# Norms moved into the expert programs, a first block with small loads only, and a result stored in eight parts

## The reference

```
def rmsnorm(x, g):
    xf = x.astype(F32)
    y = xf * lax.rsqrt(jnp.mean(xf * xf, axis=-1, keepdims=True) + EPS)
    return (y * g.astype(F32)).astype(x.dtype)
...
x -> x + mixer_i(rmsnorm(x, g[2i]))        (i = 0..3: SSD, NSA, HGRN2, SSD)
x -> x + experts_i(rmsnorm(x, g[2i+1]))
```

## Time and profile before

| | |
|---|---|
| median of three runs | 2247.63 us |
| the profiled execution, its own time | 2249.39 us |
| its span, first to last instruction | 2247.3 us |
| PE busy | 2070.9 us (92%) |
| DVE busy | 782.3 us (35%) |
| ACT busy | 593.4 us (26%) |
| mean granted clock of PE | 0.951 |
| bytes read from HBM | 600.31 MB |

### The profile page before, as it was taken

One profiled execution on the slowest core, in us unless ns is written; L12 is line 12 of the kernel. 1 busy time (PEld: TensorE's weight loads), 2 busy tenths in 40 slices (PEclk: granted clock), 3 DMA queues, 4 the chain that ended last, 5 costly groups with the idle time before them and its releaser, 6 DMA issues. The chain is left out here.

```text
span 2247.3 us, 29946 instructions
## 1 busy us (share of the span) xinstructions
PE 2070.9 (92%) x11027; PEld 1344.5 (60%) x11027; DVE 782.3 (35%) x1852; ACT 593.4 (26%) x1335; POOL 116.6 (5%) x96
## 2 busy tenths in 40 slices
PE   4999989997999768989997999989997999989998
PEld 3877854443777346754444879654443877864443
DVE  2489222222012136332222242232222489422221
ACT  2477121111111114321112332121112377221111
POOL 0133000000100000000000000000000133100000
PEclk9999999999999869999998998799998999999999
DMA  6788479997737646289996445289996688569996
GB/s 229 216 302 253 150 299 421 422 421 268 230 117 251 198 140 242 98 343 421 421 422 240 150 144 160 100 354 421 421 421 241 198 284 279 161 245 422 421 421 248
DMA packets 248711, 629.03 MB, mean 280 GB/s; under 512 B 14008, under 2 KB 175976, under 8 KB 198680
## 3 DMA queue, kind: packets, MB, share of 16 engines
q1 hardware_dynamic: 231000, 608.59, 72.7%
q10 hardware_dynamic: 15232, 10.49, 1.6%
q0 software_dynamic: 2368, 8.48, 1.1%
HBM read 600.31 MB, written 35.56 MB: 283 GB/s over the span
## 5 line engine op out<-in xcount | busy, mean ns | idle before, releaser
L1491 PE MATMUL bank<-ring,e_xg 128*64 128x512 f32 x1536 | 336.6, 594 | 0.0
L684 PE MATMUL bank<-uT,ring 128*128 128x264 f32 x1280 | 298.0, 392 | 0.0
L684 PEld LDWEIGHTS bank<-uT,ring 128*128 128x128 f32 x1280 | 243.4, 192 | 47.5 <-issue 6.8
L1491 PEld LDWEIGHTS bank<-ring,e_xg 128*64 128x64 f32 x1536 | 107.5, 137 | 211.1 <-issue 202.4
L1519 PE MATMUL bank<-e_late,e_hT 128*64 128x512 f32 x1024 | 226.8, 595 | 2.7 <-ACT e_hT L1631 2.7
L1395 DVE TENSOR_TENSOR xT<-xT,bank 128x264 f32<-128x264 f32 x256 | 109.9, 429 | 225.4 <-PE bank L1542 221.9
L1627 ACT ACT_TABLE_LOAD x32 | 41.1, 1283 | 459.5 <-PE bank L1491 459.5
L1387 DVE TENSOR_TENSOR e_hg<-e_sg,bank 128x512 f32<-128x512 f32 x32 | 22.0, 688 | 389.1 <-PE bank L1491 389.1
L1519 PEld LDWEIGHTS bank<-e_late,e_hT 128*64 128x64 f32 x1024 | 70.7, 137 | 134.8 <-issue 127.9
L2783 PE MATMUL bank<-uT,ring 128*128 128x264 f32 x512 | 124.3, 404 | 6.1 <-PEq L213 6.1
L1467 PE MATMUL bank<-e_to_row,e_u_nat 128*128 128x128 f32 x1024 | 126.1, 278 | 0.0
(11 more groups left out here) (475 smaller groups left out, 2328.1 us busy)
## 6 DMA issues: line engine op xcount, KB each, us to landing
ring<-in_moe_w SPq DMA_DIRECT2D x192, 1024.0 KB, 10.2
e_late<-in_moe_w SPq DMA_DIRECT2D x192, 1024.0 KB, 12.2
ring<-in_m_w_in SPq DMA_DIRECT2D x40, 1024.0 KB, 9.0
s_hbuf<-in_ssm SPq DMA_DIRECT2D x32, 512.0 KB, 5.5
out_ssm_s<-s_hbuf SPq DMA_DIRECT2D x32, 512.0 KB, 3.4
ring<-in_m_w_out SPq DMA_DIRECT2D x16, 1024.0 KB, 6.9
ring<-in_h_w_in SPq DMA_DIRECT2D x16, 1024.0 KB, 8.2
n_page<-in_cache_cmp SPq DMA_DIRECT2D x48, 256.0 KB, 3.9
```

The costliest lines, as they stand in the source:

```text
L684: mm = nc.tensor.matmul(bank[p % 3][0:m, 0:T], lhs, uT[:, k], start=(k == 0), stop=(k == KT - 1))
L1491: mm = nc.tensor.matmul(bank[b][CAP * j:CAP * j + CAP, :], xg[:, EK // 2 * h + k, CAP * j:CAP * j + CAP], rows_of(key)[:, k], start=(h + k ...
```

## The change

Five edits, all shown below:

1. `W.send(sp, SLOTS)` leaves the first block. It now stands in the block of the first norm, so the ring loads are issued after the small loads have landed and the barrier has been passed.
2. The block for `lb` is gone. Its instructions stand at the head of `hgrn_layer`, on DVE and ACT. The tiles `lb`, `lbm` and `lbe` are now local there.
3. `norm_all` becomes `first_norm`, for layer 0 alone. It has eight squares of one tile and a buffer of eight tiles, and a Sqrt of one column ahead of the squares, which brings Sqrt's table.
4. The norms of layers 1 to 3 stand at the end of both expert programs (`square_x` on ACT, `sum_x` on PE, `norm_x` on DVE). The square of tile c waits for the last addition to that tile.
5. In layer 3, ACT stores tile c of `xT` as a DMA of its own (132 KB), issued once its last addition is made. The last block only waits.

```diff
@@ first block @@
                 sp.dma_start(w_rt[:, 0:4 * KT * 20], I["w_rt"].rearrange("p a k c -> p (a k c)")).then_inc(*in_loaded.one())
-                W.send(sp, SLOTS)
                 sp.wait_ge(*in_loaded.now())
...
+        def first_norm():
...
+                    @block.sync
+                    def _(sp):
+                        W.send(sp, SLOTS)
+
                     @block.scalar
                     def _(act):
...
+                        nc.scalar.activation(rs[:, 0:1], eps[:, 0:1], ACT.Sqrt)
+                        for c in range(KT):
+                            nc.scalar.activation(sq[:, c], xT[:, c], ACT.Square).then_inc(*act_done.one())
+                        act.wait_ge(*pe_done.at(1))
+                        nc.scalar.activation(rs[:], bank[0][:, 0:T], ACT.Sqrt, bias=eps[:, 0:1], scale=1.0 / D).then_inc(*act_done.one())
...
@@ last block @@
-                sp.dma_start(O["yT"], xT[:]).then_inc(*out_sent.one())
-                sp.wait_ge(*out_sent.now())
+                for name in ("out_sent", "misc_dma"):
+                    sp.wait_ge(*core.count(name, 16).now())
@@ moe @@
+        def store_y(act, sent, ended):
+
+            for c in range(KT):
+                act.wait_ge(*ended(c))
+                act.dma_start(O["yT"][:, c], xT[:, c]).then_inc(*sent.one())
+
+        def square_x(act, norm, b, ended):
+
+            for c in range(KT):
+                act.wait_ge(*ended(c))
+                if c == 0:
+                    nc.scalar.activation(x_rs[:, 0:1], eps[:, 0:1], ACT.Sqrt)
+                nc.scalar.activation(x_sq[:, c], xT[:, c], ACT.Square).then_inc(*norm["x_squared"].one())
+            act.wait_ge(*norm["x_norm_step"].at(1))
+            nc.scalar.activation(x_rs[:], bank[b][:, 0:T], ACT.Sqrt, bias=eps[:, 0:1], scale=1.0 / D).then_inc(*norm["x_norm_step"].one())
+
+        def sum_x(pe, norm, b):
+
+            for c in range(KT):
+                pe.wait_ge(*norm["x_squared"].at(c + 1))
+                mm = nc.tensor.matmul(bank[b][:, 0:T], ones, x_sq[:, c], start=(c == 0), stop=(c == KT - 1))
+            mm.then_inc(*norm["x_norm_step"].one())
+
+        def norm_x(dve, norm):
+
+            dve.wait_ge(*norm["x_norm_step"].at(2))
+            nc.vector.reciprocal(x_rs[:], x_rs[:]).then_inc(*norm["x_norm_step"].one())
...
+                nc.vector.scalar_tensor_tensor(out=uT[:, c], in0=xT[:, c], scalar=par("norm_g", (layer * 2 + 2) * 8 + c), in1=x_rs[:],
+                                               op0=ALU.mult, op1=ALU.mult).then_inc(*norm["x_norm_step"].one())
...
@@ gathered_program of ACT @@
-                    leave(act, dense_total, (silu_done, comb_spread, u_copied))
+                    if layer < 3:
+                        square_x(act, norms[0], 4, lambda c: x_added.at(4 + KT * (PAIRS - 1) + c + 1))
+                    else:
+                        store_y(act, y_sent[0], lambda c: x_added.at(4 + KT * (PAIRS - 1) + c + 1))
+                    leave(act, dense_total, (silu_done, comb_spread, u_copied, *only(norms[1], "x_squared"), *stored(1)))
```

More of the change, by code:

```diff
@@ L346, in _ @@
                 link(nc.vector.memset(w_rt[:, 4 * KT * 20:], 0.0))
[L347 to L369, removed]
@@ L392, in _ @@
                             pe.wait_ge(*act_done.at(c + 1))
[L393 to L396, removed]
+                            mm = nc.tensor.matmul(bank[0][:, 0:T], ones, sq[:, c], start=(c == 0), stop=(c == KT - 1))
+                        mm.then_inc(*pe_done.one())
@@ L1264, in moe @@
         comb_made = count("comb_made")
+        y_sent = [count("out_sent", 16), count("misc_dma", 16)]
+        norms = [{name: count(f"{name}_{way}") for name in ("x_squared", "x_norm_step")} for way in ("gathered", "dense")]
         dense_total = {h_filled: 4 * NE, y_filled: 8 * NE, comb_turned: 1, silu_done: 4 * NE, h_used: 4 * NE + 2, weighted: 4 * NE + 2,
@@ L1270, in moe, with only, stored @@
                           to_row_ready: PAIRS - 1, comb_done: 7, dec_gathered: 2, dec_kept: 2, xg_copied: 2 * PAIRS}
+        if layer < 3:
+            x_sq = sb("x_sq", [128, KT, T])
+            x_rs = sb("x_rs", [128, T])
+            for c, total in (("x_squared", KT), ("x_norm_step", KT + 3)):
+                gathered_total[norms[0][c]] = dense_total[norms[1][c]] = total
+        if layer == 3:
+            for way, totals in zip(y_sent, (gathered_total, dense_total)):
+                totals[way] = 16 * KT
+        def store_y(act, sent, ended):
[3 more added lines that the diff above has]
+        def square_x(act, norm, b, ended):
+            for c in range(KT):
+                act.wait_ge(*ended(c))
[5 more added lines that the diff above has]
+        def sum_x(pe, norm, b):
+            for c in range(KT):
+                pe.wait_ge(*norm["x_squared"].at(c + 1))
[4 more added lines that the diff above has]
+            nc.vector.reciprocal(x_rs[:], x_rs[:]).then_inc(*norm["x_norm_step"].one())
+            dve.wait_ge(*norm["x_norm_step"].at(3))
+            for c in range(KT):
+                nc.vector.scalar_tensor_tensor(out=uT[:, c], in0=xT[:, c], scalar=par("norm_g", (layer * 2 + 2) * 8 + c), in1=x_rs[:],
+                                               op0=ALU.mult, op1=ALU.mult).then_inc(*norm["x_norm_step"].one())
+        def only(norm, *names):
+            return tuple(norm[name] for name in names) if layer < 3 else ()
+        def stored(way):
+            return (y_sent[way],) if layer == 3 else ()
         def leave(eng, totals, counts):
@@ L2955, in keep_rows @@
                     nc.scalar.copy(oT[:, 2 * j:2 * j + 2, 0:LP], bank[3 + j][:].rearrange("p (h t) -> p h t", h=2)).then_inc(*o_kept.one())
+                act.wait_ge(*lb_dve.at(5))
+                nc.scalar.activation(lbe[:], lbe[:], ACT.Exp).then_inc(*lb_act.one())
                 for p in range(VT + 1):
@@ L3061, in update @@
                     add.then_inc(*s_done.one())
+                bound = linker(dve, lb_dve)
+                lbv = par("h_lb", 0, 32)
+                bound(V.tensor_reduce(lbm[:], lbv.rearrange("p (l c) -> p c l", l=4), AX.X, ALU.max))
+                for l in range(4):
+                    bound(V.tensor_tensor(lbe[:, 8 * l:8 * l + 8], lbv[:, 8 * l:8 * l + 8], lbm[:], ALU.subtract))
+                dve.wait_ge(*lb_act.at(1))
+                bound(V.tensor_reduce(lbm[:], lbe[:].rearrange("p (l c) -> p c l", l=4), AX.X, ALU.add))
+                bound(V.reciprocal(lbm[:], lbm[:]))
+                bound(V.tensor_tensor(lb[:, 0:8], lbe[:, 8:16], lbe[:, 16:24], ALU.add))
+                bound(V.tensor_tensor(lb[:, 0:8], lb[:, 0:8], lbm[:], ALU.mult))
+                bound(V.tensor_scalar(lb[:, 8:16], lb[:, 0:8], -1.0, 1.0, ALU.mult, ALU.add))
                 for h in range(HH):
```

55 lines of the change are left out of this document (29 added, 26 removed).

## The result

| | before | after |
|---|---|---|
| median of four runs | 2247.74 us | 2211.57 us (2209.80 to 2214.05) |
| the profiled execution | 2249.39 us | 2212.78 us |
| its span | 2247.3 us | 2210.9 us |
| mean granted clock of PE | 0.951 | 0.951 |

The ratio after to before is 0.9839, with a 95% interval of 0.9823 to 0.9854. The forecast was 2213.7 us, 2.1 above the median.

A forecast was written before the change was run, and what follows sets the result against it. PE was taken to bound the expert blocks, so only its idle pieces, 98.8 us, could shrink. Gains of 12.5 (start), 16.8 (passages) and 4.6 (end) sum to 33.9 us: 2213.7 us from the median 2247.63, with 2205 to 2225 for 8 in 10.

The forecast's parts named there:

- The start: Before layer 0: PE's first mixer matmul starts at 24.0 us instead of 36.57, a gain of 12.5 us.
- the ends: First norm: its eight sum matmuls on PE take between 3.83 us and 6.0 us, depending on the clock.
- The rival that SP holds the first block: At the start: issuing the ring takes SP 16.81 us wherever it stands; start gains 8.1, time 2218.1 us; chance 0.14.
- The passages: Three ways from experts to the next mixer: 5.5, 5.5 and 5.8 us gained, together 16.8 us.
- Only DVE's branch is late now; PE, ACT and SP wait at the barrier. I take 3.2: Between DVE's norm and the next mixer: leaving the expert block, branch and barrier, still costs 3.2 us.
- the way out vanishes: Leaving the expert blocks: DVE's branch is served while PE sums; passages gain 25 us, time 2205.5 us; chance 0.06.
- The lower end for one passage: One passage from experts to mixer: at least 3.7 us gained, with 3.74 and 0.4 paid and 1 us more at half clock.
- The end: Behind the last addition: eight stores by ACT end the span at 2242.7 instead of 2247.3 us, a gain of 4.6 us.
- The mixers: Mixer blocks of all layers: no lengthening counted; zero taken for late conv0, at worst 2 us.
- A mixer's block is longer than before by more than 1 or 2 us: Mixer blocks in the profile after: a sign named in advance that would show the prediction wrong.
- The sum: Whole kernel: gains of 12.5, 16.8 and 4.6 us make 33.9 us, giving 2213.7 us against the median.
- my own case: Whole kernel: the main forecast of 33.9 us gained, 2213.7 us against the median; chance 0.74.

The follow-up runs named there:

- the repeat: The changed kernel run once more with nothing altered; 2214.57 us, ratio 0.9848 to the kernel before.
- store_only: The kernel before with only the result stored in eight parts by ACT; 2246.03 us, ratio 0.9986 to the kernel before.
- act_leaves_last: The changed kernel with ACT waiting, before it leaves the expert program, for DVE's last tile of the norm; 2211.54 us.
- norms_only: The kernel before with only the norms of layers 1 to 3 moved into the expert programs; 2229.65 us, ratio 0.9914 to the kernel before.
- after_pe_without_dense: The changed kernel with PE's part of the dense program, never run on these inputs, left out; 2215.44 us, ratio 0.9849 to the kernel before.
- pe_without_dense: The kernel before with PE's part of the dense program, never run on these inputs, and its branch left out; 2239.7 us, ratio 0.9952.

## Why the prediction was right, and where it was not

**The start** (12.5 forecast, 12.4 found, 11.3 in the repeat's trace): right in its steps. Small loads in by 10.5, issues that no longer take 16.8 us, a sum of 5.7 us between the ends, PE at 24.2. The rival that SP holds the first block is refuted: six issues took 11.59. Their queue was empty at the first, which fits; no run tested the queue alone.

**The passages** (16.8 forecast, 26.2 found): the failed step is "Only DVE's branch is late now; PE, ACT and SP wait at the barrier. I take 3.2". It takes the 3.74 of before for DVE's. Those were PE's branch (542.48 to 546.83 in the trace before), which now runs under PE's own sums and DVE's reciprocal, and DVE's own branch isn't late either: it comes 2.7 us before its last tile. What is left is 0.39 us. It was the rival "the way out vanishes", given 0.06, for a reason close to the right one: what is served early is PE's branch too, not only DVE's. The lower end for one passage, 3.7, should have been 3.6 by its own terms (561.40 less 552.7, 3.74, 0.4 and 1). The rest of the term held: the norm of DVE ended 8.8 us behind the additions, the sums ran without a gap, and the mixer began slow as expected (0.74 in its first 10 us), though behind 6.1 us of idle time and not 9.

**The end** (4.6 forecast, 4.4 found): the size is right. The eight stores overlapped: 132 KB each and 5.15 us for all issues, SP waiting 0.5 at the end. The rule that stood against the edit, from the Trainium skill (DMA: Bandwidth & Descriptors, Measured and Anatomy of one DMA), is DMAs of at least 1 MB and 2.0 us of fixed cost for each, measured there with DMAs that GpSimd issues. The trace does not show that cost paid one after the other. The 2.7 us that the prediction gave ACT for its branch and barrier were PE's: before, PE's branch ended at 2240.99; now ACT's takes 0.05 us, and PE, whose branch ends at 2209.43, is the last that the last block waits for, by 0.2 us over ACT.

**The mixers** (no cost forecast): wrong. "A mixer's block is longer than before by more than 1 or 2 us" was named as what would disprove me, and NSA's is longer by 5.4 us. The prediction took every mixer's length as fixed, and that is the step that failed. It is the clock: with the same 469 DVE instructions of NSA set side by side, each step of over 0.5 us by which after falls behind lies in one of its stretches at 1.2 GHz or within 3 us behind it. The table gives, for some kernels, the time that PE spent at 1.2 GHz within that layer (its length times one less the granted clock, doubled), beside the layer's length.

| | NSA at 1.2 GHz | NSA | HGRN2 at 1.2 GHz | HGRN2 |
|---|---|---|---|---|
| store_only | 109 | 650.7 | 47 | 479.5 |
| act_leaves_last | 89 | 648.8 | 62 | 484.4 |
| before | 91 | 647.6 | 64 | 486.7 |
| after | 114 | 652.9 | 70 | 488.7 |
| norms_only | 115 | 653.9 | 69 | 488.1 |
| after_pe_without_dense | 118 | 659.9 | 70 | 488.7 |

HGRN2 follows the clock closely, 9.2 us over 23 more at half rate. NSA follows it loosely (7 us between 114 and 118), since it matters what lies in a slow stretch: in the first 27.0 us of the longest (770.7 to 797.7 in after) PE is busy 13.0. The code of these layers is the same except for `lb` at HGRN2's head, which `norms_only` does not move.

Is it the shorter passage that lowers the clock? `pe_without_dense` says no: its passages take 13 us, and its NSA 653.0. The 14 us that begin 256 us behind NSA's first matmul, for before, after and `pe_without_dense`:

```profile
817.40:831.40 14.00, 13.47 (x90) 8.41 (x92) 4.39 (x12) 3.19 (x5) 0.00 (x0) 0.76 0.07 24
796.16:810.16 14.00, 11.98 (x57) 8.01 (x56) 4.00 (x6) 1.60 (x3) 0.00 (x0) 0.50 0.00 0
814.13:828.13 14.00, 11.98 (x56) 8.13 (x56) 4.00 (x6) 1.92 (x6) 0.00 (x0) 0.50 0.00 1
```

The repeat and `norms_only` show 0.50 there as well. Nor is it pure chance of an execution. Counted from NSA's first matmul, the repeat's stretches at 1.2 GHz begin and end within 0.2 us of after's. `act_leaves_last`, with passages as short as 9.6, has others, and took 648.8. The runs of one kernel do spread: before's went from 2243.13 us at a clock of 0.953 to 2254.85 at 0.945. That is 1.5 us for each 0.001 of clock, for the same program. So the loss is the clock's, it does not hang on the length of the passage, and what puts the slow stretches where they are stays open.

**The sum**: forecast 33.9, found 36.4 in span. The two errors, 9.4 us too little for the passages and 6.7 lost in the mixers, have opposite signs. The total was right within 2.5 us partly by luck, and a chance of 0.74 for my own case was too high: its mechanism at the passages was not what happened.

## What to carry to other kernels

At the end of a block, ask for each engine when it leaves and how long its own branch takes, and let the one with the longest branch leave first. Here ACT leaving last added 0.4 to 0.8 us to a passage, and PE 4.1 to 4.4. And where PE idles ahead of a stage that it bounds, unread matmuls can pay, as long as they wait for nothing that would hold its branch and no other engine's late data takes the gain back. A sum of terms that comes out can still hide terms that did not: check each one.

## What the runs showed of the hardware

- PE's branch over the skipped program takes 3.3 to 4.6 us, ACT's and DVE's 0.04 to 0.06. It runs while PE's queued matmuls still execute, and DVE's ran 2.7 us ahead of its last tile.
- Six issues of 1 MB loads took 11.59 us from an empty queue and 16.81 behind six small loads.
- An issue by ACT took 0.34 to 0.51 us for seven of the eight stores of after, and 1.57 for the seventh.
- 12 unread matmuls (5.5 us of PE) bring PE's mixer from a granted clock of 0.74 to 1.00 in its first 10 us.
- Counted from NSA's first matmul, the slow stretches of two executions of one program lay within 0.2 us of each other.
- The same program ran at mean clocks from 0.945 to 0.953 and took 2254.85 to 2243.13 us: a spread of 0.5%, more than some of the edits gave.
